# Overflow expert blocks worked in three tiles of 32 rows, and four y buffers in place of two

## The chip, the cores and the metric

The kernel runs on one core of a Trainium2 chip. TensorE (PE) multiplies, VectorE (DVE), ScalarE (ACT) and GpSimd (POOL) work beside it, SyncE (SP) only issues transfers, and 16 DMA engines carry them. The metric is the device time of one launch in microseconds; lower is better.

## The reference

One layer of a hybrid encoder for 1024 prompt rows and 32 sample rows: a token mixer, attention over 256 memory rows, and a mixture of experts with 32 experts. Everything is float32. The change touches the last part only, which is:

```
h  = silu(xr @ w_gate[e]) * (xr @ w_up[e])       # xr: rows of one block, 1024 wide; h: 512 wide
yb = h @ w_down[e]                               # 1024 wide
y  = zeros.at[tok].add(yb * gate)                # each row goes to its top-2 experts
x  = layer_norm(alpha * x + y)
```

Each of the 1056 rows goes to two experts, with a routing that depends on the data.

## The kernel before

**Blocks.** Every expert e = 0..31 gets one block of C = 96 rows, that is NS = 3 tiles of 32 rows. Rows beyond 96 of an expert go to overflow ("spilled") blocks of the same size, of which there can be up to 22. With these inputs there are two, called block 32 (j = 0) and block 33 (j = 1) here. A block needs w_gate, w_up and w_down of its expert, 2 MB each.

**What runs on each engine.** The order is written out by hand, engine by engine, with semaphores between them; each engine works its list strictly in order.

- PE, `step`: gate_up(e), 192 matmuls of the trace (L785), then down(e-1), 96 of them (L794). The output of gate_up takes two PSUM banks, 0 and 1 or 2 and 3 by parity (`B_U`), that of down banks 4 and 5 or 6 and 7 (`B_Y`). Down waits for `h_ready` from DVE.
- ACT, `act_step`: one Exp over the three tiles of gate_up(e) (L1284), then `y_rows(e-1)`: wait until down is done and until the y buffer is free (`y_out`), three scalings of 128x256 (`scale_y`, L1263), four stores to DRAM (`store_y`, L1268). There are two y buffers, so block e waits for the stores of block e-2.
- DVE, `dve_expert`: transposes x of block e+1 (L1756), then four operations of silu over 128x384 (L1743, L1745, L1747, L1749) and one transposition (L1753), which releases down(e).
- SP: loads of gate and up of e+2 when gate_up(e) is done, of down of e+2 when down(e) is done (L1002, L1003, L1007).
- POOL gathers the x rows of a block from DRAM.

**The overflow blocks** come after block 31, each engine in a function `spilled(j, b)` under an `If`. PE: gate_up(b), then the wait for `o_h`, then down(b). ACT waits first, ahead of block 32, for all y stores of the 32 experts; then per block: Exp over three tiles (L1306), wait for down, scale, store, wait until the stores have landed, one small copy (L1313). DVE as in the main loop. SP: gate and up of block 32 when gate_up(30) is done, of block 33 when gate_up(31) is done; down of each when down(30) or down(31) is (L1028, L1029, L1034).

**After them** ACT signals `fin_ready` (L1326). POOL then gathers every row's two y rows from DRAM (L1967), and the last layer norm follows tile by tile.

```
act.wait_ge(y_done, e + 1)
act.wait_ge(gate_ready, e + 1)
wait_count(act, y_out[b], 64 * j)
scale_y(b).then_inc(y_ready, 1)
act.wait_ge(y_ready, e + 1)
store_y(y_dram[bass.ds(e * C, C), :], b, y_out[b], 16)
```

Of the kernel before, what the change touches and what calls it, by code (L numbers as in the profile page):

```python
# [23 lines left out]
NE = G * EG  # L24
DE = 512
KE = DE // P
C = 96
NS = C // 32
# [4 lines left out]
BANK = 512  # L33
# [16 lines left out]
def build(nc, io):  # L50
    ctx = ExitStack()
    with ctx:
        def sem(name):
            return ctx.enter_context(nc.semaphore(name))
# [46 lines left out]
        gate2 = const(2 * NS).rearrange("p (b a) -> p b a", a=NS)  # L101
# [7 lines left out]
        R = MIX + KD * T  # L109
# [70 lines left out]
        gu = [view(a, "m k n", m=2, k=KD, n=DE) for a in EXP]  # L180
        wd = [view(a + 8192, "k n", k=KE, n=D) for a in EXP]
# [92 lines left out]
        y_out = [sem(f"y_out{i}") for i in range(2)]  # L274
# [5 lines left out]
        o_gate = sem("o_gate")  # L280
# [125 lines left out]
        def _(pe):  # L406
            mm = nc.tensor.matmul
# [418 lines left out]
            pe.wait_ge(tables_ready, 1)  # L826
            n_over = pe.value_load(over_i[0:1, NOVER:NOVER + 1], min_val=0, max_val=NOVER)

            def spilled(j, b, turn_n):
                pe.wait_ge(o_xt, j + 1)  # L830
                pe.wait_ge(o_w[b], 32 * turn_n + 32)
                gate_up(b).then_inc(o_gu, 1)
                pe.wait_ge(o_h, j + 1)
                pe.wait_ge(o_down[b], 16 * turn_n + 16)
                if isinstance(j, int):
                    pe.wait_ge(y_ready, NE - 1 + j)
                else:
                    pe.wait_ge(o_y, 65 * j - 129)
                down(b).then_inc(o_dn, 1)

            with pe.If(n_over > 0):
                spilled(0, 0, 0)
# [10 lines left out]
        def _(sp):  # L853
# [168 lines left out]
            def spilled(j, b):  # L1022
                e = sp.value_load(over_i[0:1, bass.ds(j, 1)], min_val=0, max_val=NE - 1)
                if isinstance(j, int):
                    sp.wait_ge(gu_done, NE - 1 + j)
                else:
                    sp.wait_ge(o_gu, j - 1)
                sp.dma_start(gu[b][:, 0], dyn(gate_w, e)).then_inc(o_w[b], 16)  # L1028
                sp.dma_start(gu[b][:, 1], dyn(up_w, e)).then_inc(o_w[b], 16)  # L1029
                if isinstance(j, int):  # L1030
                    sp.wait_ge(y_done, NE - 1 + j)
                else:
                    sp.wait_ge(o_dn, j - 1)
# [19 lines left out]
            sp.wait_ge(mem_out, 16)  # L1053
            for i in range(2):
                sp.wait_ge(state_out[i], 32 * HH // 2)
                sp.wait_ge(y_out[i], 64 * NE // 2)


        @block.scalar
        def _(act):  # L1060
# [200 lines left out]
            def scale_y(b):  # L1261
                for a in range(NS):
                    last = A(ye[:, b, a, :], B_Y[b][:, a * 256:(a + 1) * 256], ACT.Copy, scale=gate2[:, b, a:a + 1])  # L1263
                return last

            def store_y(rows, b, s, n):
                for q in range(4):
                    act.dma_start(rows[:, 256 * q:256 * q + 256].rearrange("(a t) n -> t a n", t=32),  # L1268
                                  ye[32 * q:32 * q + 32, b]).then_inc(s, n)

            def y_rows(e, b, j):

                act.wait_ge(y_done, e + 1)
                act.wait_ge(gate_ready, e + 1)
                wait_count(act, y_out[b], 64 * j)
                scale_y(b).then_inc(y_ready, 1)
                act.wait_ge(y_ready, e + 1)
                store_y(y_dram[bass.ds(e * C, C), :], b, y_out[b], 16)

            def act_step(e, b, j, first=False):  # L1280
                act.wait_ge(gu_done, e + 1)
                if not first:
                    act.wait_ge(h_ready, e)
                A(sg, gate_rows[b], ACT.Exp, scale=-1.0).then_inc(g_exp, 1)  # L1284
                if not first:
                    y_rows(e - 1, 1 - b, j + b - 1)

            act_step(0, 0, 0, first=True)
            act_step(1, 1, 0)
            act_step(2, 0, 1)  # L1290
            with act.Fori(1, NE // 2 - 1) as i:
                act_step(2 * i + 1, 1, i)
                act_step(2 * i + 2, 0, i + 1)
            act_step(NE - 1, 1, NE // 2 - 1)
            y_rows(NE - 1, 1, NE // 2 - 1)

            act.wait_ge(tables_ready, 1)
            n_over = act.value_load(over_i[0:1, NOVER:NOVER + 1], min_val=0, max_val=NOVER)

            def spilled(j, b):  # L1300
                act.wait_ge(o_gu, j + 1)
                if isinstance(j, int) and j == 0:
                    act.wait_ge(h_ready, NE)
                else:
                    act.wait_ge(o_h, j)
                A(sg, gate_rows[b], ACT.Exp, scale=-1.0).then_inc(g_exp, 1)  # L1306
                act.wait_ge(o_dn, j + 1)
                act.wait_ge(o_gate, j + 1)
                scale_y(b).then_inc(o_y, 1)
                act.wait_ge(o_y, 65 * j + 1)  # L1310
                store_y(y_dram[bass.ds(j * C + NE * C, C), :], b, o_y, 16)
                act.wait_ge(o_y, 65 * j + 65)
# [8 lines left out]
            with act.If(n_over > 2):  # L1321
                with act.Fori(1, NOVER // 2) as i:
                    for b in range(2):
                        with act.If(2 * i + b < n_over):
                            spilled(2 * i + b, b)
            A(rstd[:, 1:2], eps_ln, ACT.Copy).then_inc(fin_ready, 1)  # L1326

            for t in range(NT):
# [13 lines left out]
        def _(dve):  # L1342
# [409 lines left out]
            def turn_h(b):  # L1752
                return V.transpose(hhT[:, b], hh.rearrange("p s (d k) -> p s k d", k=KE))  # L1753
# [34 lines left out]
            def spilled(j, b, turn_n):  # L1788
                dve.wait_ge(o_x[b], 16 * NS * turn_n + 16 * NS)
                turn_x(b).then_inc(o_xt, 1)  # L1790
                dve.wait_ge(g_exp, j + NE + 1)
                silu_up(b, 4 * j + 4 * NE)
                if isinstance(j, int):
                    dve.wait_ge(y_done, NE - 1 + j)
                else:
                    dve.wait_ge(o_dn, j - 1)
                turn_h(b).then_inc(o_h, 1)
                if isinstance(j, int):
                    dve.wait_ge(y_ready, NE - 1 + j)
                else:  # L1800
                    dve.wait_ge(o_y, 65 * j - 129)
# [204 lines left out]
```

## Time and profile before

| | us |
|---|---|
| median of 3 runs | 1997.67 (1995.52 to 1998.9) |
| the profiled execution | 1996.47 |
| its span on the core | 1994.1 |
| PE busy | 1792.5 (90%) |
| DVE busy | 750.0 (38%) |
| ACT busy | 309.1 (16%) |

Times in rows are microseconds from the start of the span. "<-" behind an idle time names what ended it. The transfers' GB/s and the share of the 16 DMA engines say whether the memory side is full: over the expert stage, from about 1360 to 1885, it is.

### The profile page before, as it was taken

The numbers are of one execution on the slowest core, as the hardware profiler recorded it, in microseconds if no ns is written. First come the engines' busy times: TensorE is split into PE (matmuls) and PEld (weight loads), VectorE is DVE, ScalarE is ACT, GpSimd is POOL, SyncE is SP. The second block draws the span as 40 slices with busy tenths as digits, with TensorE's granted clock in tenths as the row PEclk, the third lists the DMA queues.
The fourth block names the chain that finished last, engine by engine and source line by source line (L and its number), as shares of the span: only waits on it lengthen the run. The fifth ranks groups of instructions, "written<-read, shape, count | busy, mean of one in ns | idle before, by whom it ended". The sixth has DMA issues, their size and how long they took to land. (4 is left out here: it accounts for less than half of the span.)

```text
span 1994.1 us, 33667 instructions
## 1 busy us (share of the span) xinstructions
PE 1792.5 (90%) x14867; PEld 1131.6 (57%) x14867; DVE 750.0 (38%) x1089; ACT 309.1 (16%) x701; POOL 210.5 (11%) x196
## 2 busy tenths in 40 slices
PE   8999999999999779999998999939999999999650
PEld 4455568766654554445665665426666666666420
DVE  1111456534461653320012443364433333333227
ACT  1111223411010440111001111000101111111005
POOL 2100000000010420000000000032111111111016
PEclk9999999999999689999999999859999999999875
DMA  5341002001100203045111000349999999999826
GB/s 197 96 165 43 1 5 83 1 1 43 42 0 4 92 6 116 33 136 169 34 42 42 22 22 28 144 171 366 422 424 424 424 425 423 424 424 424 360 61 216
DMA packets 72862, 326.94 MB, mean 164 GB/s; under 512 B 13368, under 2 KB 27968, under 8 KB 59728
## 3 DMA queue, kind: packets, MB, share of 16 engines
q1 hardware_dynamic: 47840, 280.70, 35.1%
q10 hardware_dynamic: 17360, 22.03, 3.4%
q0 software_dynamic: 7584, 23.08, 3.2%
q8 instruction: 61, 1.00, 0.2%
q14 instruction: 17, 0.14, 0.0%
HBM read 288.05 MB, written 37.65 MB: 163 GB/s over the span
## 5 line engine op out<-in xcount | busy, mean ns | idle before, releaser
L785 PE MATMUL psum<-arena 128*32 128x256 f32 x6528 | 360.4, 380 | 32.0 <-issue 30.8
L418 PE MATMUL psum<-arena 128*128 128x352 f32 x1152 | 342.1, 460 | 0.0
L785 PEld LDWEIGHTS psum<-arena 128*32 128x32 f32 x6528 | 244.7, 110 | 146.5 <-issue 45.4
L427 PE MATMUL psum<-arena 128*128 128x512 f32 (+1 forms) x720 | 318.4, 601 | 5.9 <-DMA arena<-in_w_in 4.7
L418 PEld LDWEIGHTS psum<-arena 128*128 128x128 f32 x1152 | 219.3, 191 | 122.2 <-issue 1.1
L1348 DVE COPY arena<-psum 128x512 f32<-128x512 f32 (+7 forms) x135 | 90.9, 681 | 417.8 <-PE psum L427 221.6
L427 PEld LDWEIGHTS psum<-arena 128*128 128x128 f32 (+1 forms) x720 | 131.7, 185 | 177.4 <-issue 175.5
L794 PE MATMUL psum<-arena 128*32 128x256 f32 x3264 | 189.7, 389 | 24.1 <-DVE arena L1753 24.1
L794 PEld LDWEIGHTS psum<-arena 128*32 128x32 f32 x3264 | 125.4, 113 | 82.0 <-DVE arena L1753 25.5
L1743 DVE TENSOR_SCALAR arena<-arena 128x384 f32<-128x384 f32 x34 | 12.2, 360 | 357.1 <-ACT arena L1284 315.3
L1065 ACT ACTIVATE arena<-psum 128x128 f32<-128x128 f32 (+5 forms) x181 | 86.5, 495 | 349.8 <-PE psum L411 276.2
L1938 POOL DMA_INDIRECT arena<-x_rows,consts x102 | 96.7, 948 | 414.1 <-DVE arena L1756 386.0
L411 PE MATMUL psum<-consts,arena 128*128 128x128 f32 (+4 forms) x819 | 121.8, 280 | 12.4 <-ACT arena L1065 6.3
L411 PEld LDWEIGHTS psum<-consts,arena 128*128 128x128 f32 (+4 forms) x819 | 97.2, 154 | 59.0 <-issue 30.8
L643 PE MATMUL psum<-arena 128*128 128x512 f32 (+1 forms) x288 | 125.3, 593 | 0.0
L1545 DVE SCALAR_TENSOR_TENSOR arena<-arena,psum 128x1024 f32<-128x1024 f32 (+1 forms) x18 | 22.0, 1220 | 185.8 <-PE psum L427 103.8
L1263 ACT ACTIVATE arena<-psum,consts 128x256 f32<-128x256 f32 x102 | 40.9, 471 | 324.0 <-DMA y_blocks<-arena 270.6
L643 PEld LDWEIGHTS psum<-arena 128*128 128x128 f32 (+1 forms) x288 | 51.5, 181 | 68.3 <-issue 67.9
L1745 DVE RECIPROCAL arena<-arena 128x384 f32<-128x384 f32 x34 | 86.8, 2553 | 1.2
L546 PE MATMUL psum<-arena 128*128 128x64 f32 (+2 forms) x624 | 76.5, 266 | 0.0
L511 PE MATMUL psum<-arena 66*128 66x512 f32 (+3 forms) x192 | 75.6, 502 | 0.5 <-DVE consts L1348 0.5
L1118 ACT ACTIVATE arena<-psum,consts 128x128 f32<-128x128 f32 (+8 forms) x72 | 51.3, 713 | 150.5 <-DVE consts L1401 148.7
(243 smaller groups left out, 1402.1 us busy)
## 6 DMA issues: line engine op xcount, KB each, us to landing
arena<-in_moe_w_down SPq DMA_DIRECT2D x34, 2048.0 KB, 22.6
arena<-in_moe_w_gate SPq DMA_DIRECT2D x34, 2048.0 KB, 16.9
arena<-in_moe_w_up SPq DMA_DIRECT2D x34, 2048.0 KB, 22.0
arena<-in_w_in SPq DMA_DIRECT2D x7, 2048.0 KB, 9.8
y_blocks<-arena ACTq DMA_DIRECT2D x136, 96.0 KB, 2.0
y_blocks<-arena ACTq DMA_DIRECT2D x1, 8448.0 KB, 44.0
arena<-in_x_prompt SPq DMA_DIRECT2D x9, 512.0 KB, 3.3
arena<-in_w_out SPq DMA_DIRECT2D x2, 2048.0 KB, 11.0
```

What stands on the lines that cost most here:

```text
L411: return nc.tensor.transpose(out, a, ident[0:n, 0:n])
L418: last = mm(ps[0:m, c * BANK:c * BANK + THIRD], lhs(k), rhs[:, k, c * THIRD:(c + 1) * THIRD], start=(k == 0), stop=(k == KD - 1))
L427: last = mm(ps[0:n, c * 512:(c + 1) * 512], lhs(k), rhs(k, c), start=(k == 0), stop=(k == KD - 1))
L511: last = mm(ps[0:nq, c:e], q, ka[0:KX, h, c:e], start=True, stop=True)
L546: last = mm(ps_o[0:nq, h * FD:(h + 1) * FD], probsT[p][0:w_, u % nbuf, b, 0:nq], v, start=(b == 0), stop=(b == len(blocks) - 1))
L643: last = mm(psum[0:n, b:b + BANK], mixT[:, k, cols_of(t)], wrows[:, k, c * 512:(c + 1) * 512], start=(k == 4), stop=(k == 3))
L785: last = mm(out, xeT[:, b, a, k, :], gu[b][:, :, k, j * P:(j + 1) * P], start=(k == 0), stop=(k == KD - 1))
L794: last = mm(B_Y[b][32 * j:32 * j + 32, a * 256:(a + 1) * 256], hhT[:, b, a, k, :], wd[b][:, k, j * 256:(j + 1) * 256], start=(k == 0), sto ...
L1065: take(A(out, src, ACT.Copy), key)
L1348: take(V.tensor_copy(out, src), key)
L1745: V.reciprocal(sg, sg).then_inc(silu_step, 1)
L1938: pool.indirect_dma_start(out=xe[:, b, a, :], out_offset=None, in_=x2_quarters, in_offset=bass.IndirectOffsetOnAxis(ap=tok_idx[:, e, a:a + ...
```

## The change

**Main loop.** Four y buffers `ye[0..3]` in place of two; block e uses buffer e % 4 and waits for the stores of block e-4. ACT's loop is unrolled by four experts instead of two. Nothing else moves in the main loop.

**Overflow blocks.** Each of the three tiles of gate_up has a bank of its own (3b + a) and its own signal `o_gu`. ACT takes Exp tile by tile (128x128), DVE does the silu and the transposition tile by tile and signals `o_h` three times a block; its small copy of the gate values (L1802 before) now stands ahead of the silu. PE's down waits per tile, writes all blocks' results to banks 6 and 7 (`O_Y`, tiles 0 and 1 in bank 6, tile 2 in bank 7), and signals `o_dn` after tile 1 and after tile 2. ACT scales tiles 0 and 1 after the first signal and tile 2 after the second. The wait for all y stores of the experts moves from ahead of the overflow blocks to behind them; a block waits only for the buffer that it uses. The wait for a block's own stores (`o_out`) stays at the block's end.

```diff
-        ye = view(R + 15360, "a s n", a=2, s=NS, n=256)
+        ye = [view(R + a, "s n", s=NS, n=256) for a in (15360, 16128, 21504, 22272)]
...
             def spilled(j, b, turn_n):
                 pe.wait_ge(o_xt, j + 1)
                 pe.wait_ge(o_w[b], 32 * turn_n + 32)
-                gate_up(b).then_inc(o_gu, 1)
-                pe.wait_ge(o_h, j + 1)
-                pe.wait_ge(o_down[b], 16 * turn_n + 16)
...
+                for a in range(NS):
+                    for k in range(KD):
+                        for q in range(4):
+                            out = psum[32 * q:32 * q + 32, (3 * b + a) * BANK:(3 * b + a) * BANK + 256]
...
+                    last.then_inc(o_gu, 1)
+                pe.wait_ge(o_down[b], 16 * turn_n + 16)
...
+                for a in range(NS):
+                    pe.wait_ge(o_h, 3 * j + a + 1)
...
+                    if a > 0:
+                        last.then_inc(o_dn, 1)
...
             def spilled(j, b):
-                act.wait_ge(o_gu, j + 1)
...
+                for a in range(NS):
+                    act.wait_ge(o_gu, 3 * j + a + 1)
+                    A(sg[:, a, :], psum[:, (3 * b + a) * BANK:(3 * b + a) * BANK + P], ACT.Exp, scale=-1.0)\
+                        .then_inc(g_exp, 1)
                 act.wait_ge(o_gate, j + 1)
...
-            for i in range(2):
-                act.wait_ge(y_out[i], 64 * (NE // 2))
             with act.If(n_over > 0):
                 spilled(0, 0)
```

**How the lists differ.** ACT, from the end of the main loop through the first overflow block. Before, with the branch into block 32 behind the stores of both buffers:

```order
L1263 ACTIVATE arena<-psum,consts 128x256 [waits y_out1,gate_ready,y_done]
L1263 ACTIVATE arena<-psum,consts 128x256 x2
L1268 DMA y_blocks<-arena 32x3x256 [waits y_ready]
L1268 DMA y_blocks<-arena 32x3x256 x3
L1298 TENSOR_LOAD consts [waits tables_ready]
L1298 ISA x2
L1317 COMPARE_AND_BRANCH [waits y_out1,y_out0]
L1306 ACTIVATE arena<-psum 128x384 [waits h_ready,o_gu]
```

The same place in the changed kernel:

```order
L1289 ACTIVATE arena<-psum,consts 128x256 [waits y_out3,gate_ready,y_done]
L1289 ACTIVATE arena<-psum,consts 128x256 x2
L1280 DMA y_blocks<-arena 32x3x256 [waits y_ready]
L1280 DMA y_blocks<-arena 32x3x256 x3
L1312 TENSOR_LOAD consts [waits tables_ready]
L1312 ISA x2
L1338 COMPARE_AND_BRANCH
L1323 ACTIVATE arena<-psum 128x128 [waits o_gu,h_ready]
L1323 ACTIVATE arena<-psum 128x128 [waits o_gu] x2
L1330 ACTIVATE arena<-psum,consts 128x256 [waits y_out0,o_dn,o_gate]
```

The wait on y_out has left the branch and stands on the first scaling; the Exp is in three parts.

PE, the first overflow block, before and now:

```order
-L785 MATMUL psum<-arena 32x256 [waits o_w0,o_xt]
-L785 MATMUL psum<-arena 32x256 x95
-L794 MATMUL psum<-arena 32x256 [waits y_ready,o_down0,o_h]
-L794 MATMUL psum<-arena 32x256 x47
```

```order
+L840 MATMUL psum<-arena 32x256 [waits y_ready,o_w0,o_xt]
+L840 MATMUL psum<-arena 32x256 x95
+L852 MATMUL psum<-arena 32x256 [waits o_h,y_ready,o_down0]
+L852 MATMUL psum<-arena 32x256 x15
+L852 MATMUL psum<-arena 32x256 [waits o_h]
+L852 MATMUL psum<-arena 32x256 x15
+L852 MATMUL psum<-arena 32x256 [waits o_h]
+L852 MATMUL psum<-arena 32x256 x15
```

The matmuls and their order are the same (each of the listing is two MATMULs of the trace); the wait for `o_h` stands at three places instead of one.

## Rows read from the trace of the kernel before

**Rows 1.** Busy time by stretch: length, engines, granted clock, DMA share, GB/s.

```profile
1600.00:1700.00 100.00, 94.53 (x1736) 67.16 (x1732) 38.64 (x42) 9.44 (x23) 17.04 (x19) 1.00 1.01 424
...
1864.00:1866.00 2.00, 0.00 (x0) 0.00 (x0) 1.90 (x4) 0.00 (x0) 0.00 (x0) 0.65 1.10 438
...
1886.00:1888.00 2.00, 0.00 (x0) 0.00 (x0) 0.00 (x0) 0.13 (x1) 0.00 (x0) 1.00 0.29 106
...
1890.00:1892.00 2.00, 0.00 (x0) 0.00 (x0) 0.00 (x0) 0.00 (x0) 0.00 (x0) 0.50 0.89 192
```

**Rows 2.** DMA queues, 1500 to 1533.32: packets, MB, share; q1 SP's, q10 ACT's.

```profile
q1 hardware_dynamic: 864, 12.58, 88.8%
q10 hardware_dynamic: 864, 0.76, 6.6%
```

**Rows 3.** Timeline of PE, the end of the expert stage: start, duration, what.

```profile
1845.85 10.57 PE L785 MATMUL psum<-arena 128*32 128x256 f32 x192 [1.18 <-DMA arena<-in_moe_w_up]
1856.21 5.39 PE L794 MATMUL psum<-arena 128*32 128x256 f32 x96
1866.40 7.84 PE L794 MATMUL psum<-arena 128*32 128x256 f32 x96 [4.80 <-DVE arena L1753]
1874.07 10.53 PE L785 MATMUL psum<-arena 128*32 128x256 f32 x192
1898.22 7.30 PE L794 MATMUL psum<-arena 128*32 128x256 f32 x96 [13.62 <-DVE arena L1753]
1905.34 10.54 PE L785 MATMUL psum<-arena 128*32 128x256 f32 x192
1921.55 7.58 PE L794 MATMUL psum<-arena 128*32 128x256 f32 x96 [5.67 <-DVE arena L1753]
```

**Rows 4.** Timeline of ACT, two places of the expert stage and its end.

```profile
1478.54 1.20 ACT L1263 ACTIVATE arena<-psum,consts 128x256 f32<-128x256 f32 x3 [5.05 <-DMA y_blocks<-arena]
...
1860.80 0.49 ACT L1284 ACTIVATE arena<-psum 128x384 f32<-128x384 f32 x1 [2.17 <-issue]
1875.15 1.20 ACT L1263 ACTIVATE arena<-psum,consts 128x256 f32<-128x256 f32 x3 [13.86 <-DMA y_blocks<-arena]
...
1892.63 0.49 ACT L1306 ACTIVATE arena<-psum 128x384 f32<-128x384 f32 x1 [3.56 <-DMA y_blocks<-arena]
...
1934.95 0.20 ACT L1326 ACTIVATE consts<-consts 128x1 f32<-128x1 f32 x1
```

**Rows 5.** Groups of DVE instructions by shape: busy us, mean ns.

```profile
L1745 DVE RECIPROCAL arena<-arena 128x384 f32<-128x384 f32 x34 | 86.8, 2553 | 1.2
L1756 DVE STREAM_TRANSPOSE arena<-arena 128x768 f32<-128x768 f32 x34 | 54.3, 1596 | 8.5 <-DMA arena<-x_rows,consts 8.3
L1753 DVE STREAM_TRANSPOSE arena<-arena 128x384 f32<-128x384 f32 x34 | 30.0, 883 | 1.2
L1439 DVE RECIPROCAL arena<-arena 128x1056 f32<-128x1056 f32 x4 | 27.0, 6753 | 0.1
...
L1400 DVE TENSOR_TENSOR psum<-psum,consts 128x128 f32<-128x128 f32 x64 | 19.1, 298 | 61.5 <-PE psum L511 61.5
...
L1743 DVE TENSOR_SCALAR arena<-arena 128x384 f32<-128x384 f32 x34 | 12.2, 360 | 357.1 <-ACT arena L1284 315.3 <-ACT arena L1306 41.8
```

**Rows 6.** SP's loads of w_up for blocks 32 and 33: issues, and the second's landing.

```profile
1847.40 0.38 SPq L1029 DMA_DIRECT2D arena<-in_moe_w_up  x1
...
1863.29 1.53 SPq L1029 DMA_DIRECT2D arena<-in_moe_w_up  x1
...
DMA to landing us min/median/max: 19.6/19.6/19.6
```

**Rows 7.** SP early on, timeline: a load and a store behind others.

```profile
90.04 0.55 SPq L894 DMA_DIRECT2D arena<-in_w_in  x1
...
93.34 22.33 SPq L900 DMA_DIRECT2D out_fox_k_s<-arena  x1
```

**Rows 8.** DMA issues between 80 and 135: that first load of them, KB, us to landing.

```profile
arena<-in_w_in SPq DMA_DIRECT2D x1, 2048.0 KB, 29.6
```

More of the change, by code:

```diff
@@ L273, in build @@
         xe_in = [sem(f"xe_in{i}") for i in range(2)]
-        y_out = [sem(f"y_out{i}") for i in range(2)]
+        y_out = [sem(f"y_out{i}") for i in range(4)]
         gu_done, y_done = sem("gu_done"), sem("y_done")
@@ L831, in spilled @@
                 pe.wait_ge(o_w[b], 32 * turn_n + 32)
-                gate_up(b).then_inc(o_gu, 1)
-                pe.wait_ge(o_h, j + 1)
-                pe.wait_ge(o_down[b], 16 * turn_n + 16)
                 if isinstance(j, int):
                     pe.wait_ge(y_ready, NE - 1 + j)
-                else:
-                    pe.wait_ge(o_y, 65 * j - 129)
-                down(b).then_inc(o_dn, 1)
+                for a in range(NS):
+                    for k in range(KD):
+                        for q in range(4):
+                            out = psum[32 * q:32 * q + 32, (3 * b + a) * BANK:(3 * b + a) * BANK + 256]
+                            last = mm(out.rearrange("p (m n) -> p m n", m=2), xeT[:, b, a, k, :],
+                                      gu[b][:, :, k, q * P:(q + 1) * P], start=(k == 0), stop=(k == KD - 1))
+                    last.then_inc(o_gu, 1)
+                pe.wait_ge(o_down[b], 16 * turn_n + 16)
+                if isinstance(j, int) and j == 0:
+                    pe.wait_ge(y_ready, NE)
+                else:
+                    pe.wait_ge(o_y, j)
+                for a in range(NS):
+                    pe.wait_ge(o_h, 3 * j + a + 1)
+                    for k in range(KE):
+                        for q in range(4):
+                            last = mm(O_Y[32 * q:32 * q + 32, a * 256:(a + 1) * 256], hhT[:, b, a, k, :],
+                                      wd[b][:, k, q * 256:(q + 1) * 256], start=(k == 0), stop=(k == KE - 1))
+                    if a > 0:
+                        last.then_inc(o_dn, 1)
             with pe.If(n_over > 0):
@@ L1055, in _ @@
                 sp.wait_ge(state_out[i], 32 * HH // 2)
-                sp.wait_ge(y_out[i], 64 * NE // 2)
+            for i in range(4):
+                sp.wait_ge(y_out[i], 64 * NE // 4)
         @block.scalar
@@ L1259, in _, with store_y @@
                          for a in (0, 2)]
[L1261 to L1266, printed above, removed]
+            def store_y(rows, slot, s):
                 for q in range(4):
                     act.dma_start(rows[:, 256 * q:256 * q + 256].rearrange("(a t) n -> t a n", t=32),
-                                  ye[32 * q:32 * q + 32, b]).then_inc(s, n)
@@ L1271, in y_rows @@
-            def y_rows(e, b, j):
+                                  ye[slot][32 * q:32 * q + 32]).then_inc(s, 16)
+            def y_rows(e, b, slot, turn_n):
                 act.wait_ge(y_done, e + 1)
                 act.wait_ge(gate_ready, e + 1)
-                wait_count(act, y_out[b], 64 * j)
-                scale_y(b).then_inc(y_ready, 1)
+                wait_count(act, y_out[slot], 64 * turn_n)
+                for a in range(NS):
+                    last = A(ye[slot][:, a, :], B_Y[b][:, a * 256:(a + 1) * 256], ACT.Copy, scale=gate2[:, b, a:a + 1])
+                last.then_inc(y_ready, 1)
@@ L1277, in y_rows, with act_step @@
                 act.wait_ge(y_ready, e + 1)
-                store_y(y_dram[bass.ds(e * C, C), :], b, y_out[b], 16)
-            def act_step(e, b, j, first=False):
+                store_y(y_dram[bass.ds(e * C, C), :], slot, y_out[slot])
+            def act_step(e, r, turn_n):
                 act.wait_ge(gu_done, e + 1)
-                if not first:
+                if not isinstance(e, int) or e > 0:
                     act.wait_ge(h_ready, e)
-                A(sg, gate_rows[b], ACT.Exp, scale=-1.0).then_inc(g_exp, 1)
-                if not first:
-                    y_rows(e - 1, 1 - b, j + b - 1)
@@ L1288, in _ @@
[L1288 to L1295, printed above, removed]
+                A(sg, gate_rows[r % 2], ACT.Exp, scale=-1.0).then_inc(g_exp, 1)
+                if not isinstance(e, int) or e > 0:
+                    y_rows(e - 1, (r - 1) % 2, (r - 1) % 4, turn_n)
@@ L1297, in _ @@
+            for e in range(7):
+                act_step(e, e % 4 + 4, (e - 1) // 4)
+            with act.Fori(1, NE // 4 - 1) as i:
+                for r in range(3, 7):
+                    act_step(4 * i + r, r, i if r < 5 else i + 1)
+            act_step(NE - 1, NE - 1, NE // 4 - 1)
+            y_rows(NE - 1, 1, 3, NE // 4 - 1)
             act.wait_ge(tables_ready, 1)
             n_over = act.value_load(over_i[0:1, NOVER:NOVER + 1], min_val=0, max_val=NOVER)
+            O_Y = psum[:, 6 * BANK:8 * BANK]
@@ L1304, in spilled @@
                 else:
-                    act.wait_ge(o_h, j)
-                A(sg, gate_rows[b], ACT.Exp, scale=-1.0).then_inc(g_exp, 1)
-                act.wait_ge(o_dn, j + 1)
-                act.wait_ge(o_gate, j + 1)
[L1309 to L1312, printed above, removed]
+                    act.wait_ge(o_h, 3 * j)
+                for a in range(NS):
+                    act.wait_ge(o_gu, 3 * j + a + 1)
+                    A(sg[:, a, :], psum[:, (3 * b + a) * BANK:(3 * b + a) * BANK + P], ACT.Exp, scale=-1.0)\
+                        .then_inc(g_exp, 1)
+                act.wait_ge(o_gate, j + 1)
+                act.wait_ge(o_dn, 2 * j + 1)
+                if isinstance(j, int):
+                    act.wait_ge(y_out[b], 64 * NE // 4)
+                for a in range(2):
+                    A(ye[b][:, a, :], O_Y[:, a * 256:(a + 1) * 256], ACT.Copy, scale=gate2[:, b, a:a + 1])
+                act.wait_ge(o_dn, 2 * j + 2)
+                A(ye[b][:, 2, :], O_Y[:, 512:768], ACT.Copy, scale=gate2[:, b, 2:3]).then_inc(o_y, 1)
+                act.wait_ge(o_y, j + 1)
+                store_y(y_dram[bass.ds(j * C + NE * C, C), :], b, o_out)
+                act.wait_ge(o_out, 64 * j + 64)
                 A(lnv[:, 0:1], eps_ln, ACT.Copy)
-            for i in range(2):
-                act.wait_ge(y_out[i], 64 * (NE // 2))
             with act.If(n_over > 0):
@@ L1325, in _ @@
                             spilled(2 * i + b, b)
+            for i in range(4):
+                act.wait_ge(y_out[i], 64 * NE // 4)
             A(rstd[:, 1:2], eps_ln, ACT.Copy).then_inc(fin_ready, 1)
```

31 lines of the change are left out of this document (20 added, 11 removed).

## Prediction

> **What bounds the kernel now.** I read the busy time by stretch first. Over the expert stage the 16 DMA engines are full (share 1.01) at 424 GB/s, and 1736 matmuls in 100 us are 6.03 experts of 288, so 16.6 us each [rows 1]. PE is busy 94.5% of it and waits for weights only. A block moves 6.29 MB of weights, 0.39 MB of y and about as much of x: 7.08 MB / 424 GB/s is 16.7 us. The main loop is bound by bytes, and the change moves none of them. I count no gain there, though the chain of waits puts y stores first.
>
> Then the timeline of PE. From the end of gate_up(31) at 1856.4 its three idle stretches are 4.80, 13.62 and 5.67 us, all ended by DVE's transposition of h [rows 3]. The timeline of ACT says why. Block 28's stores land only at 1875.15, block 5's landed at 1478.54: 396.6 us for 23 blocks, so a set of stores is served every 17.2 us, while blocks come every 16.6 [rows 1, 4]. With two buffers ACT falls behind; it takes Exp(31) at 1860.80, 4.4 us after gate_up(31). Then it holds Exp(32) until every y store has landed, 1892.63, though gate_up(32) was done at 1884.6. The end of the path is `fin_ready` at 1934.95; from it 59.15 us of gathers and layer norm follow to 1994.1, and 2.37 us lie outside the span.
>
> **How the y stores are served.** In 33.32 us the queue of ACT got exactly as many packets as that of SP, 864 and 864 [rows 2]. Its 0.76 MB are 1.93 sets of 0.393 MB, so a set is 447 packets, 28 for each engine, and takes 17.2 us, which agrees with the landings. So the y queue gets one packet for each weights packet, however many sets stand in it. I take it that blocks 28 and 29 land when they did, and the sets queued behind them only after the weights.
>
> The Trainium skill, page "DMA: Bandwidth & Descriptors", section "Queues, rings and completion order", says that each DMA engine goes round robin over the queues that have work, a packet at a time. The trace agrees, 864 to 864. By this rule a deeper y queue gets no larger share, which speaks against this change; were the shares by need instead, block 32's stores would land some 2 us after their issue, and the sum would be the 1967 of the first rival.
>
> **Part by part, from 1856.4 on.**
>
> 1. Four buffers. Exp(31) no longer waits. DVE then takes Exp 0.5 us and silu 5.0 us (for block 31: Exp at 1860.80, down(31) at 1866.40, 5.6 us in all [rows 3, 4]). H is there at 1862.1, down(31) starts 0.5 us after down(30), at 1862.1. PE pauses 0.5 instead of 4.8 us. In that pause the granted clock fell, 0.65 of full in 1864 to 1866 [rows 1], and down(31) took 7.84 us where 5.39 is the time at 2.4 GHz [rows 1, 3]. In the main loop pauses of 0.9 us leave the clock at 1.00, so I take 5.39 (5.18 from start to start, the last matmul overlapping). Down(31) ends at 1867.5: 6.7 us gained.
>
> 2. Gate_up(32) needs x turned (DVE 1.6 us behind the silu, 1863.9) and w_up of block 32, which was issued at 1847.40 and, if it takes the 19.6 us of the next one, lands at 1867.0 [rows 6]. Both are there. It ends at 1877.9, 6.7 us early.
>
> 3. Tiles. Per tile DVE pays, by the 384- and 1056-column rows of the reciprocal, 2553 - 256 x 6.25 = 953 ns; the two products 298 each by the 128-column row; the scalar addition at most 360, some 230; the transposition between 883/3 and 883, by the slope to 768 columns 408 [rows 5]. With gaps 2.33 us. A tile of gate_up takes 3.45 us of PE, so only the last one's chain is open: 0.2 + 0.3 (Exp) + 2.33 = 2.8 us after gate_up. Down's first two tiles cover 3.45 us of that. Down(32) then follows at once: 13.6 us of idle time and 2.1 us of slow clock go [rows 3]. It would end at 1883.1 instead of 1905.4.
>
> 4. Issue of the stores. More sets now stand in ACT's queue. Before, at most two did, 56 packets for each engine, and no issue was held. When block 31 is issued, at 1871, there are 3.1 (served by then: up to part of 28). Early in the kernel such a queue does fill: SP had two transfers of 64 packets for each engine in its queue and was held 22.33 us in the third, until 115.67, with the first landing at 119.64 [rows 7, 8]. So the queue takes about 64 to 72 packets for each engine beyond which the issue is held. Block 31's last of four stores needs 88 - 7 = 81 to fall to 64 or 72: 9 to 17 packets at 1.6 per us are 5 to 10 us. ACT comes to Exp(32) at 1876 to 1881 instead of 1871; silu of three tiles follows, 7.3 us, and down(32) ends at 1885.4 to 1890.6. The row is of another queue; zero is the lower end. I take 1887.
>
> 5. Gate_up(33) needs w_up of block 33, landing at 1863.29 + 19.6 = 1882.9 [rows 6], and x turned, which comes with the last tile of h. It runs 1887 to 1897.5 in my middle case.
>
> 6. The new wait that counts: ACT does Exp(33) only when block 32's own stores have landed (`o_out`), as before, but now blocks 29 to 32 stand in the queue when the weights end at about 1886. Three and a half sets at 106 to 192 GB/s, the rates just behind the weights and of block 31's alone [rows 1], beside each other some 6 to 10 us: landing at 1892.5 to 1896. I take 1893.5. Exp at that time, the three tiles of silu one after another, 7.3 us, and the last tile of down 1.8 us: 1902.6; by gate_up(33) itself 1897.5 + 2.8 + 1.8 = 1902.1. The two delays of 4 and 6 cover each other. With half a microsecond for clock, down(33) ends at 1903.2, against 1929.1 [rows 3].
>
> 7. Scaling: one of three scalings stays behind the last matmul: 0.8 us gained (1.20 to 0.47 by the row of three [rows 4]). The stores and their landing are as before.
>
> Sum: 25.9 + 0.8 = 26.7 us. 1996.47 - 26.7 = 1969.8; the median of the runs shown is 1.2 higher, so **1971**. Costed at nothing: SP's loads (only down(33) is issued earlier, and it queues behind w_up), ACT's longer loop body, the moved copy on DVE (its two waits are met at 1863 and 1869), and the final waits on y_out, met by then. If PE's down found its weights late it would show: w_down of 33 is needed at 1897 and lands by 1888.
>
> **The rivals.**
>
> - No delay of the y stores (steps 4 and 6 cost nothing): gate_up(33) from 1883.1 to 1893.6, down(33) ends at 1898.2 to 1899.2. That is 4 us less, **1967**. For it: ACT's queue never showed a held issue, and step 6's rate is only bounded. Against: the equal packet counts. Chance 0.17.
> - The queue holds only two sets, as much as the trace shows in it: block 31's stores go in at about 1886, when the weights end. Then Exp(32) at 1886, down(32) ends 1895.3, gate_up(33) 1905.7, down(33) 1910.3: 7.1 us more, **1978**. In the main loop ACT would then be held in the issue instead of the wait. Chance 0.15.
> - The tiles don't overlap: the waits stand in PE's list but h comes late, so that 5.6 us stay behind each gate_up. Against it is DVE's 2.33 us a tile against PE's 3.45. With the clock then slow in both downs, 2 x 5.6 + 4.4 less the cover of step 6 leaves about 10 us more: **1981**, with the rival before 1987. Chance 0.06.
> - Slower than before: ACT no longer lags, so x, y and weights all want the DMA engines at the same time throughout, and each block's period grows. The price of the gain is 26.7 us over some 26 blocks of a full loop, so it decides from 1.03 us a block, 6%, or 0.44 MB of extra traffic at 424 GB/s, more than a whole set of y a block. With twice that, **2024**. Against: the y queue is never empty before either, and bytes don't change. At most the two sets that come earlier cost 2 us once. Chance 0.03.
>
> **How the numbers follow.** The forecast 1971 has 0.57 (its own span 1968 to 1975), the rivals 0.17, 0.15, 0.06 and 0.03, and 0.02 are for nothing gained. 1964.5 to 1979 takes in the forecast, the first two rivals with 2 us for the loop, and leaves out 0.11 and some of the tails. A run of this kernel can tell 0.2%, 4 us: faster 0.95, same 0.02, slower 0.03.
>
> **What the profile would show.** ACT's Exp of every block 0.2 us after its gate_up, down(31) within 1 us of down(30) and 5.4 us long, the main loop still 16.6 us a block. Down(32) directly behind gate_up(32) is step 3 without step 4; a store issue of several us in ACT at 1870 is step 4. ACT's first Exp of block 33 after a wait for a DMA at 1892 to 1896 is step 6. I am wrong if the period in the loop moves by more than 0.1 us, if block 32's stores land before 1889 or after 1898, or if the granted clock is not 1.00 up to gate_up(33).

## The result and the profile after

| | before | after |
|---|---|---|
| median, us | 1998.29 (4 runs) | 1970.38 (4 runs: 1967.48 to 1971.37) |
| ratio | | 0.9856, 95% interval 0.9844 to 0.9868 |
| profiled execution, us | 1996.47 | 1967.48 |
| its span, us | 1994.1 | 1965.7 |
| end of gate_up(31), from the span's start | 1856.4 | 1856.8 |
| `fin_ready` | 1934.95 | 1907.07 |
| from there to the end | 59.15 | 58.63 |

The kernel is 1.4% faster, 27.9 us by the medians. In the two profiled executions `fin_ready` comes 27.9 us earlier, and up to the end of gate_up(31) nothing has moved by more than 0.4 us. So the gain lies between two points of the program that were 78.5 us apart and are 50.3 now.

The busy time by stretch in the middle of the main loop, with the columns of [rows 1]:

```profile
1600.00:1700.00 100.00, 94.55 (x1736) 67.24 (x1732) 38.63 (x42) 10.15 (x24) 17.09 (x19) 1.00 1.01 424
```

This is the first line of [rows 1] over again: 1736 matmuls in 100 us, DMA full at 424 GB/s. The queues of SP and ACT, 1500 to 1533.32, still get equal counts of packets, to be laid beside [rows 2]:

```profile
q1 hardware_dynamic: 865, 12.60, 88.9%
q10 hardware_dynamic: 865, 0.76, 6.6%
```

The end of the expert stage is where the two traces differ. PE's timeline, from gate_up(31) on, to be laid beside [rows 3]; L840 is gate_up and L852 down of an overflow block:

```profile
1846.19 10.57 PE L785 MATMUL psum<-arena 128*32 128x256 f32 x192 [1.19 <-DMA arena<-in_moe_w_up]
1856.55 5.39 PE L794 MATMUL psum<-arena 128*32 128x256 f32 x96
1862.42 5.39 PE L794 MATMUL psum<-arena 128*32 128x256 f32 x96 [0.48 <-DVE arena L1776]
1867.63 10.54 PE L840 MATMUL psum<-arena 128*32 128x256 f32 x192
1879.19 1.93 PE L852 MATMUL psum<-arena 128*32 128x256 f32 x32 [1.02 <-DVE arena L1833]
1881.28 1.93 PE L852 MATMUL psum<-arena 128*32 128x256 f32 x32 [0.15 <-DVE arena L1833]
1883.46 1.93 PE L852 MATMUL psum<-arena 128*32 128x256 f32 x32 [0.24 <-DVE arena L1833]
1885.21 10.54 PE L840 MATMUL psum<-arena 128*32 128x256 f32 x192
1895.57 5.36 PE L852 MATMUL psum<-arena 128*32 128x256 f32 x96
```

The idle stretches of 4.80, 13.62 and 5.67 us are 0.48, 1.41 (in three parts) and none. The three downs that took 7.3 to 7.8 us take 5.4, or three times 1.93, because the clock no longer falls; in the stretch that holds the pause before down(31) it is granted in full, where [rows 1] had 0.65:

```profile
1862.00:1864.00 2.00, 1.57 (x32) 0.98 (x36) 1.48 (x3) 1.20 (x3) 0.00 (x0) 1.00 1.00 422
```

ACT's timeline of the same stretch, to be laid beside [rows 4]: L1299 is Exp(31), L1280 the store issues, L1323 Exp of a tile, L1336 the small copy behind a block's own stores.

```profile
1856.82 0.49 ACT L1299 ACTIVATE arena<-psum 128x384 f32<-128x384 f32 x1 [10.55 <-PE psum L785]
...
1863.23 2.98 ACTq L1280 DMA_DIRECT2D y_blocks<-arena  x4
...
1869.11 6.37 ACTq L1280 DMA_DIRECT2D y_blocks<-arena  x4
1876.44 0.45 ACT L1323 ACTIVATE arena<-psum 128x128 f32<-128x128 f32 x2 [7.35 <-issue]
1878.24 0.28 ACT L1323 ACTIVATE arena<-psum 128x128 f32<-128x128 f32 x1 [1.36 <-PE psum L840]
...
1891.46 0.20 ACT L1336 ACTIVATE consts<-consts 128x1 f32<-128x1 f32 x1 [5.53 <-DMA y_blocks<-arena]
...
1895.82 0.28 ACT L1323 ACTIVATE arena<-psum 128x128 f32<-128x128 f32 x1 [3.18 <-PE psum L840]
...
1906.44 0.20 ACT L1336 ACTIVATE consts<-consts 128x1 f32<-128x1 f32 x1 [4.97 <-DMA y_blocks<-arena]
1907.07 0.20 ACT L1349 ACTIVATE consts<-consts 128x1 f32<-128x1 f32 x1 [0.42 <-issue]
```

Exp(31) follows its gate_up at once. The four issues of block 31's stores take 6.37 us, one of them 4.53. Exp(32) comes at 1876.44, 5 us after its first tile was there. The wait for block 32's own stores ends at 1891.5, but the last tile's Exp waits for PE alone.

### The profile page after: what moved, and what is told of

The parts are those of the page before. It is cut to its first block and busy times, and to the rows that moved or that the text cites. A ratio compares the mean times of both kernels' runs of the same rounds, so it can differ in the third digit from the quotient of the medians.

```text
span 1965.7 us, 33639 instructions
## 1 busy us (share of the span) xinstructions
PE 1787.5 (91%) x14867; PEld 1130.0 (57%) x14867; DVE 756.5 (38%) x1109; ACT 309.8 (16%) x705; POOL 209.9 (11%) x196
## 5 line engine op out<-in xcount | busy, mean ns | idle before, releaser
L785 PE MATMUL psum<-arena 128*32 128x256 f32 x6144 | 339.3, 380 | 31.9 <-issue 30.7
L785 PEld LDWEIGHTS psum<-arena 128*32 128x32 f32 x6144 | 232.0, 110 | 138.1 <-issue 45.1
L794 PE MATMUL psum<-arena 128*32 128x256 f32 x3072 | 172.4, 379 | 0.5 <-DVE arena L1776 0.5
L794 PEld LDWEIGHTS psum<-arena 128*32 128x32 f32 x3072 | 117.2, 110 | 49.3 <-DVE arena L1776 1.0
L1768 DVE RECIPROCAL arena<-arena 128x384 f32<-128x384 f32 x32 | 81.7, 2553 | 1.1
L546 PEld LDWEIGHTS psum<-arena 128*128 128x128 f32 (+2 forms) x624 | 72.5, 186 | 2.3 <-issue 1.0
```

Source lines behind the costliest of these rows:

```text
L546: last = mm(ps_o[0:nq, h * FD:(h + 1) * FD], probsT[p][0:w_, u % nbuf, b, 0:nq], v, start=(b == 0), stop=(b == len(blocks) - 1))
L1768: V.reciprocal(sg, sg).then_inc(silu_step, 1)
```

## The experiments

Eleven kernels beside the one on trial. Times are medians; the kernel before was measured beside each group, at 1998.1 to 1998.8.

| kernel | us | ratio to before, 95% interval |
|---|---|---|
| buffers only | 1994.4 | 0.9973 (0.9947 to 0.9998) |
| buffers, moved wait, no tiles | 1985.2 | 0.9930 (0.9913 to 0.9946) |
| tiles and moved wait, two buffers | 1985.3 | 0.9932 (0.9915 to 0.9949) |
| the whole change, early wait put back | 1983.8 | 0.9923 (0.9906 to 0.9939) |
| the whole change, three buffers | 1975.2 | 0.9877 (0.9860 to 0.9895) |
| the whole change | 1970.4 | 0.9856 (0.9841 to 0.9871) |
| own stores waited for later | 1969.8 | 0.9856 (0.9841 to 0.9871) |
| block 31's stores from SP | 1969.9 | 0.9855 (0.9840 to 0.9870) |
| both | 1967.4 | 0.9843 (0.9829 to 0.9856) |
| both, block 33's stores from two queues | 1965.0 | 0.9832 (0.9819 to 0.9846) |
| block 29's stores left out | 1968.5 | one execution |
| the stores of blocks 4 to 27 left out | 1946.8 | 0.9746 (0.9731 to 0.9760) |

### The four buffers alone

The main loop of the changed kernel, the overflow blocks of the one before.

```diff
-            for i in range(2):
-                act.wait_ge(y_out[i], 64 * (NE // 2))
+            for i in range(4):
+                act.wait_ge(y_out[i], 64 * (NE // 4))
             with act.If(n_over > 0):
                 spilled(0, 0)
```

> The kernel before with the four y buffers and ACT's new main loop, and nothing else: the overflow blocks whole, behind the wait for all y stores. Theory (the gain is at the end of the expert stage, and the loop is bound by bytes): down(31) starts 0.5 us after down(30) and gate_up(32) ends at about 1878, but Exp(32) still waits for block 31's stores, landing at about 1890, where it was 1892.6: some 3 us faster than before, 1995, and the period of the main loop unchanged at 16.6 us. Rival (the y stores at the head of the chain of waits are what bounds the loop): most of the 28 us come with the buffers, 1972 to 1980.

Measured: 1994.4. The first line is of its chain of waits, the others of PE and ACT:

```profile
PE 36%; DVE 4%; issue 2%; DMA 2%; POOL 1%; ACT 0%; ACTq 0%; DVEq 0%; SPq 0%; POOLq 0%
```

```profile
1867.79 10.57 PE L785 MATMUL psum<-arena 128*32 128x256 f32 x192
1896.40 6.90 PE L794 MATMUL psum<-arena 128*32 128x256 f32 x96 [18.04 <-DVE arena L1753]
```

```profile
1890.81 0.49 ACT L1304 ACTIVATE arena<-psum 128x384 f32<-128x384 f32 x1 [21.81 <-DMA y_blocks<-arena]
```

In the kernel before, the chain's first item was DMA with 21%, all of it y_blocks. Here that item is gone from the chain; and the time fell by 4 us, since gate_up(32) came 6 us earlier and then waited 18 us. The stores were at the head of the chain because ACT always had one to wait for, not because anything waited for ACT. The rival falls.

### Two buffers, with the tiles

```diff
-        ye = [view(R + a, "s n", s=NS, n=256) for a in (15360, 16128, 21504, 22272)]
+        ye = [view(R + a, "s n", s=NS, n=256) for a in (15360, 16128)]
```

> The changed kernel with two y buffers and the main loop of before: the tiles and the moved wait alone. Theory: ACT still lags, Exp(31) at 1860.8, block 31's scaling waits for block 29's stores until 1887.9, so Exp(32) comes at about 1891, h of its last tile 7.3 us later, down(32) ends at 1900, gate_up(33) at 1910.4, down(33) at 1915: 14 to 15 us faster than before, 1984. Rival (the buffers add nothing to the tiles): 1970, as the whole change.

Measured: 1985.3, as expected. ACT comes to Exp(32) when block 31's stores have at last been issued:

```profile
1887.05 1.20 ACT L1280 ACTIVATE arena<-psum,consts 128x256 f32<-128x256 f32 x3 [12.62 <-DMA y_blocks<-arena]
1888.28 1.77 ACTq L1285 DMA_DIRECT2D y_blocks<-arena  x4
1891.00 0.61 ACT L1326 ACTIVATE arena<-psum 128x128 f32<-128x128 f32 x3 [2.75 <-issue]
```

### The buffers and the moved wait, without tiles

```diff
-            for i in range(4):
-                act.wait_ge(y_out[i], 64 * (NE // 4))
             with act.If(n_over > 0):
...
                 act.wait_ge(o_gate, j + 1)
+                if isinstance(j, int):
+                    act.wait_ge(y_out[b], 64 * NE // 4)
```

> Four buffers and the moved wait, the overflow blocks whole as before. Theory: Exp(32) follows gate_up(32) at 1878.2, silu takes 5.0 us in one piece, down(32) starts at 1883.7, gate_up(33) ends at 1899.6, down(33) starts at 1905.2 and ends at 1910.6 to 1912.8 by its clock: 16 to 18 us faster than before, 1981, so that the tiles are worth about 10 us of the whole. Rival (the tiles add only instructions, the waits were the cost): 1971.

Measured: 1985.2, 4 us more than expected. PE's two downs of the overflow blocks:

```profile
1885.22 7.91 PE L794 MATMUL psum<-arena 128*32 128x256 f32 x96 [5.65 <-DVE arena L1755]
...
1909.15 7.89 PE L794 MATMUL psum<-arena 128*32 128x256 f32 x96 [5.66 <-DVE arena L1755]
```

The pauses are those that were expected, the durations are not: both downs are slow, 2.5 us each, where the expectation counted a slow clock in the second at most. gate_up(31) also starts 1 us later in this execution than in the changed kernel's, for reasons ahead of the change. The tiles are thus worth 14.8 us on top of the rest: 11.3 us of pauses less the 1.4 that stay, and 5.0 of clock.

### The early wait put back

```diff
+            for i in range(4):
+                act.wait_ge(y_out[i], 64 * NE // 4)
             with act.If(n_over > 0):
                 spilled(0, 0)
```

> The changed kernel with the wait for all y stores put back ahead of the overflow blocks. Theory: Exp(32) at about 1890, when block 31's stores have landed; tile by tile on DVE 7.3 us, down(32) ends at 1899.5, gate_up(33) at 1910, down(33) at 1914.5: 13 to 14 us slower than the whole change, 1984. Rival (the wait costs nothing with four buffers, since the stores would have landed): 1971.

Measured: 1983.8, 13.4 us more than the whole change. ACT's first three tiles come all at once, 21 us after its last work:

```profile
1892.96 0.61 ACT L1323 ACTIVATE arena<-psum 128x128 f32<-128x128 f32 x3 [21.07 <-DMA y_blocks<-arena]
```

The four kernels show how the parts stand to each other. Alone, the buffers bring 4 us; the tiles and the moved wait, with two buffers, bring 13; all three together 28. Take any one of the three away and 13 to 15 us are lost, so they add up to more than their single shares. The reason is that ACT reaches Exp(32) early only if it neither waits for a buffer nor for all stores.

The tiles need that least. With four buffers and the early wait they still bring 10.6 us (1994.4 to 1983.8), since the pause of 5.67 us and the slow clock ahead of down(33) go in any case; with the moved wait they bring 14.8. The moved wait brings 9.2 us without the tiles and 13.4 with them. The 4 us between these pairs are less than the 5 us to which the time with the buffers alone is known. The tiles alone, and the moved wait alone, with two buffers each, weren't run.

### Three buffers

Block 31 and both overflow blocks use the buffers of blocks 28, 29 and 30; ACT's loop is written out in full.

```diff
-                    y_rows(e - 1, (r - 1) % 2, (r - 1) % 4, turn_n)
+                    y_rows(e - 1, (e - 1) % 2, (e - 1) % 3, (e - 1) // 3)
```

> The changed kernel with three y buffers, ACT's loop written out in full. Theory: backlog is 2.5 sets in the loop, so three buffers never make ACT wait there by much; only block 31 waits, for block 28's stores landing at 1875.2, which is when its issue ended in the changed kernel anyway: within 1.5 us of the whole change, 1970 to 1972. Rival (the fourth buffer is what lets ACT run free): ACT lags in the loop and the time is 1975 or more.

Measured: 1975.2, 4.8 us slower than the whole change. The theory missed. The time is the rival's, but its mechanism isn't there: ACT didn't lag in the loop.

```profile
1879.13 1.21 ACT L1289 ACTIVATE arena<-psum,consts 128x256 f32<-128x256 f32 x3 [12.52 <-DMA y_blocks<-arena]
1880.37 2.60 ACTq L1280 DMA_DIRECT2D y_blocks<-arena  x4
1883.90 0.61 ACT L1325 ACTIVATE arena<-psum 128x128 f32<-128x128 f32 x3 [3.56 <-issue]
```

```profile
1871.04 10.54 PE L840 MATMUL psum<-arena 128*32 128x256 f32 x192
1886.65 8.23 PE L852 MATMUL psum<-arena 128*32 128x256 f32 x96 [5.07 <-DVE arena L1835]
```

In the loop ACT never waited for a buffer. For block 31 the buffer did come free when block 28's stores landed, but scaling and issue, 1.2 and 2.6 us, stand behind that, while a full queue lets the issue end as soon as there is room. Exp(32) comes 12.9 us after the start of gate_up(32), in the changed kernel 8.8. And the pause of 5.07 us costs the clock in down(32), 8.23 us instead of 5.4. The expectation left both out. So the fourth buffer serves the last block of the loop; in the loop before it nothing waited for a buffer.

### Block 29's stores left out

The y rows of block 29 are zeros here, written at the start.

```diff
-                store_y(y_dram[bass.ds(e * C, C), :], slot, y_out[slot])
+                if e != 29:
+                    store_y(y_dram[bass.ds(e * C, C), :], slot, y_out[slot])
```

> The changed kernel without the stores of block 29's y rows (they are zeros, set early), ACT's loop written out in full. With them the four issues of block 31's stores took 6.37 us. Theory (the issue is held because the queue is full, 88 packets for each engine): with 60 packets there they take 1.8 to 3 us, and Exp(32) comes at 1871 to 1873 instead of 1876.4. Rival (the issue is slow because SP issues loads at that time, or since the instructions are new there): still 6 us.

Measured in one execution, 1968.5 us:

```profile
1865.44 2.87 ACTq L1281 DMA_DIRECT2D y_blocks<-arena  x4
1870.13 1.20 ACT L1290 ACTIVATE arena<-psum,consts 128x256 f32<-128x256 f32 x3 [4.72 <-PE psum L794]
1871.37 1.79 ACTq L1281 DMA_DIRECT2D y_blocks<-arena  x4
1874.09 0.28 ACT L1326 ACTIVATE arena<-psum 128x128 f32<-128x128 f32 x1 [2.75 <-PE psum L840]
```

Block 31's issues take 1.79 us, and Exp(32) follows its tile at once. SP issues the same loads at the same time here, and the instructions are as new. What held the issue was how much stood in ACT's own queue. Whether the limit counts packets or stores stays open: in the six traces with four buffers in which ACT issued block 31's stores behind all of those before, the held issue ended 29.3 to 30.5 us behind the start of gate_up(31), and block 28's stores landed 29.3 us behind it in the kernel before and 29.5 with three buffers. Not every long issue is of this kind. Block 30's 2.87 us stand here and there, about a microsecond more than in the loop; they took 2.60 in the kernel before, which had only two buffers. Block 32's took 3.25 us, and 3.3 to 4.3 where block 29's or block 31's weren't in the queue. What these have in common the runs don't show.

### Where the two remaining delays lie

Two edits and both together. In the first, block 32's own stores are waited for only ahead of block 33's; in the second, SP issues block 31's stores behind its last loads.

```diff
-                act.wait_ge(o_out, 64 * j + 64)
...
+                if isinstance(j, int) and j == 1:
+                    act.wait_ge(o_out, 64)
                 store_y(y_dram[bass.ds(j * C + NE * C, C), :], b, o_out)
```

```diff
+            sp.wait_ge(y_ready, NE)
+            for q in range(4):
+                sp.dma_start(y_dram[(NE - 1) * C:NE * C, 256 * q:256 * q + 256].rearrange("(a t) n -> t a n", t=32),
+                             ye[3][32 * q:32 * q + 32]).then_inc(y_out[3], 16)
```

> The changed kernel itself, beside the three variants of this group: 1970 us, 28 us faster than before.

> The changed kernel with block 32's wait for its own stores moved behind block 33's scaling. Theory: the first Exp of block 33 comes at 1889 instead of 1891.6, but the last tile's Exp waits for gate_up(33) in both, so nothing is gained: within 0.5 us of the changed kernel. Rival (this wait holds the path): 2 to 3 us faster.

> The changed kernel with block 31's stores issued by SP behind its last loads, so that ACT is free at 1869. Theory (the full queue holds ACT, which holds Exp(32)): Exp(32) at 1871.3, down(32) follows gate_up(32) at once and ends at 1883.1, gate_up(33) starts at 1883.4 with w_up's landing: 1.8 us faster than the changed kernel. Rival (the held issue is hidden): no difference, or slower since these stores now stand before the output stores of SP.

> Both of the last two. Theory: with gate_up(33) 1.8 us earlier the wait for block 32's own stores comes nearer to the path, so both together give 1.8 to 2.3 us. Rival: the landing of block 32's stores was never near, and it is as the one with SP alone.

Measured: 1970.4, 1969.8, 1969.9 and 1967.4. The executions differ by 1 to 2 us ahead of the expert stage's end, so the traces are best compared from the start of gate_up(31) to the end of down(33): 54.7 and 55.5 us in two executions of the changed kernel, 55.3 with the late wait, 54.3 with SP's stores, 52.9 with both. With SP's stores alone down(32) follows gate_up(32) at once and gate_up(33) starts 37.0 us after gate_up(31), where it was 39.0 and 39.8. Then the other wait takes most of it back:

```profile
1883.30 10.54 PE L840 MATMUL psum<-arena 128*32 128x256 f32 x192
1894.46 1.93 PE L852 MATMUL psum<-arena 128*32 128x256 f32 x32 [0.62 <-DVE arena L1838]
1896.56 1.93 PE L852 MATMUL psum<-arena 128*32 128x256 f32 x32 [0.16 <-DVE arena L1838]
1898.74 1.93 PE L852 MATMUL psum<-arena 128*32 128x256 f32 x32 [0.24 <-DVE arena L1838]
```

With both edits no down waits:

```profile
1870.03 10.54 PE L840 MATMUL psum<-arena 128*32 128x256 f32 x192
1880.39 5.36 PE L852 MATMUL psum<-arena 128*32 128x256 f32 x96
1885.77 10.57 PE L840 MATMUL psum<-arena 128*32 128x256 f32 x192
1896.12 5.39 PE L852 MATMUL psum<-arena 128*32 128x256 f32 x96
```

So each delay hides the other, as step 6 of the prediction said: removing one gives 0.6 us or less, both 2 to 3. The expectation for the stores from SP, 1.8 us faster, missed: Exp(32) and gate_up(33) did come as it said, but it didn't follow the path on to down(33), which then waited 1.02 us. By the intervals the step from 1970.4 to 1967.4 is at the edge of what the timing tells, and the steps of half a microsecond are below it; the lines of the traces are the better witness.

### Block 33's stores from two queues

On top of both:

```diff
+                sp.wait_ge(o_y, 2)
+                stores(NE + 1, 1, (2, 3), o_out)
...
-                store_y(y_dram[bass.ds(j * C + NE * C, C), :], b, o_out)
+                if isinstance(j, int) and j == 1:
+                    for q in range(2):
+                        act.dma_start(y_dram[(NE + 1) * C:(NE + 2) * C, 256 * q:256 * q + 256].rearrange("(a t) n -> t a n", t=32),
+                                      ye[1][32 * q:32 * q + 32]).then_inc(o_out, 16)
```

> The variant with both edits (block 31's stores from SP, block 32's own stores waited for later), and block 33's four stores issued two by ACT and two by SP. Theory: the four issues behind the last scaling take 1.77 us in ACT, two take 0.9: another 0.9 us off, 1966.5. Rival (the landing of about 3 us behind them sets the end, whoever issues): no difference to 1967.4.

Measured: 1965.0, five of the six executions between 1963.6 and 1966.7.

```profile
1918.21 0.47 ACT L1345 ACTIVATE arena<-psum,consts 128x256 f32<-128x256 f32 x1 [0.84 <-PE psum L852]
1918.71 0.86 ACTq L1349 DMA_DIRECT2D y_blocks<-arena  x2
1921.62 0.20 ACT L1355 ACTIVATE consts<-consts 128x1 f32<-128x1 f32 x1 [2.94 <-DMA y_blocks<-arena]
```

From the last scaling's end to the copy behind the stores it is 2.94 us instead of the changed kernel's 4.97. The issues give 0.9 of that, as expected (1.77 to 0.86). The other 1.1, a shorter landing behind the last issue, can't be put down to the second queue. In the kernel with block 32's late wait, where ACT issued all four in 1.79 us, the landing was shorter still, 3.45 less 1.79:

```profile
1906.28 0.20 ACT L1339 ACTIVATE consts<-consts 128x1 f32<-128x1 f32 x1 [3.45 <-DMA y_blocks<-arena]
```

Over the thirteen traces in which ACT issued all four stores of block 33 this stretch ran from 3.45 to 5.16 us. The intervals of this kernel and of the one with both edits overlap, so the 2.4 us between the medians show a gain at most, not its size. By the median it is the fastest version with all stores, 1.7% under the kernel before.

Its profiled execution is the sixth, 1982.8 us long. Gate_up(31) starts at 1865.30 there instead of 1845 to 1850 in the others that store every block. The loss lies ahead of the expert stage, in code that no variant changes. From about 249 to 287 us the granted clock was 0.50, its lower level of 1.2 GHz, while PE was busy without a pause and nothing moved by DMA:

```profile
260.00:280.00 20.00, 20.00 (x63) 14.09 (x63) 8.72 (x20) 4.35 (x12) 0.00 (x0) 0.50 0.00 1
```

In the same stretch the changed kernel ran 108 matmuls at 1.00. Some 38 us at half the clock lose about 19 us (an estimate from these numbers), which is the delay. Why the clock fell there is open.

### The stores of blocks 4 to 27 left out

Zeros stand in their place, written at the start.

```diff
-                store_y(y_dram[bass.ds(e * C, C), :], slot, y_out[slot])
+                if not 4 <= e < 28:
+                    store_y(y_dram[bass.ds(e * C, C), :], slot, y_out[slot])
```

> The changed kernel without the stores of the y rows of blocks 4 to 27 (zeros stand there, set early), ACT's loop written out in full. Theory (the loop is bound by bytes): 6.69 MB a block at 424 GB/s are 15.8 us instead of 16.66, PE's own work is 15.6, so a period of 15.6 to 15.8 and some 20 us less over 24 blocks: 1950. The y queue is empty by block 31, so no issue is held. Rival (PE or the order of the loads sets the period): 16.66 us a block still, and 1968.

Measured: 1946.8, ratio 0.9746 (0.9731 to 0.9760), 3 us less than expected.

```profile
1600.00:1700.00 100.00, 99.61 (x1828) 70.63 (x1821) 43.88 (x49) 10.69 (x27) 17.00 (x18) 1.00 1.01 423
```

DMA is as full as before, at 423 GB/s, and 1828 matmuls pass in 100 us instead of 1736: 15.75 us a block, where 6.69 MB / 424 GB/s is 15.8. PE is busy 99.6%, so it stands at the edge of its own work. The y stores do cost the loop 0.9 us a block, by their bytes; when they are issued, or how long they take to land, costs it nothing. That is why the buffers moved nothing there. 24 blocks of 0.9 us are 22 of the 23.6 us gained. Of the rest, 1.6 to 2.4 us lie behind the start of gate_up(31), from which it is 53.1 us to the end of down(33) instead of 54.7 and 55.5: block 31's issues take 1.76 us, and down(32) follows gate_up(32) at once.

## Why the prediction was right

It forecast 1971; 1970.38 was measured, and none of its three signs of being wrong came: as many matmuls pass in 100 us of the loop, block 32's stores land at 1891.5, and the granted clock is 1.00 up to gate_up(33). The path and the mechanism are as forecast; that the number is off by only 0.6 us is in part luck, since steps 4 and 6 were too slow by 2.3 us together and step 7 too fast by 1.0. Step by step, in the changed kernel's profiled execution:

- **The loop** was costed at nothing, and its period is unchanged. Shown from both sides: by the buffers alone, 4 us, and by the stores left out.
- **Step 1**, down(31) at 1862.1 and 5.39 us long: 1862.42 and 5.39.
- **Step 2**, gate_up(32) to end at 1877.9: 1878.2.
- **Step 3**, the tiles. The costs of DVE at 128 columns were drawn from wider rows. Measured, count and mean in ns:

```profile
L1827 DVE RECIPROCAL arena<-arena 128x128 f32<-128x128 f32 x6 | 5.7, 953 | 0.2
...
L1833 DVE STREAM_TRANSPOSE arena<-arena 128x128 f32<-128x128 f32 x6 | 2.5, 412 | 0.2
...
L1829 DVE TENSOR_TENSOR arena<-arena,psum 128x128 f32<-128x128 f32 x6 | 1.7, 287 | 0.2
...
L1825 DVE TENSOR_SCALAR arena<-arena 128x128 f32<-128x128 f32 x6 | 1.2, 199 | 19.1 <-ACT arena L1323 19.1
```

  The slopes of [rows 5] gave 953, 408, 298 and 230. A tile takes 2.20 us, 2.33 was said.
- **Step 4**, the held issue, was a step that no row of this stage showed; it came from a stall of another queue at 93 us [rows 7, 8]. It is there, 6.37 us instead of 1.77, and is proved by block 29's stores left out. The size was a little high: Exp(32) at 1876.4 lies at the near end of 1876 to 1881, and down(32) ends at 1885.4, where 1887 was taken. The queue took more than the 64 to 72 packets for each engine that were estimated. By the step's own working the fourth store found 81, and 4.53 us at 1.6 packets a microsecond are 7 of them, so it was taken at some 74. Counted from the other end, if block 28's stores land just then, as they did at 1875.15 before, three sets of 28 less the 7 of the held store are 77. So the estimate from these numbers is 74 to 77 ahead of the held store. The step said that no issue was held before; that isn't quite so, since one of block 30's took 1.28 us there.
- **The service of the y queue**, one packet for each weights packet however many sets stand in it, decides whether block 29's stores land as before. They were issued from 1846.4 to 1847.9, 12 us before their issue in the kernel before, and the last landed 40.5 us behind (the third number), so at 1888.4, against 1887.9. This supports the step but doesn't prove it: the first of the four is put at 19.0 us, 1865.4, ahead of the 1875.15 at which block 28's landed before, and no run settles that:

```profile
DMA to landing us min/median/max: 19.0/25.1/40.5
```

- **Step 6**, block 32's own stores: landing at 1891.5, where 1893.5 was taken. Its sum doesn't come out: three and a half sets, 1.38 MB, at 106 to 192 GB/s are 7 to 13 us and not 6 to 10. The measured rate was higher, 267, 225 and 56 GB/s in the three stretches of 2 us from 1886 on. The wait held up only the first tile's Exp of block 33. The step said that the two delays cover each other; they do, and this one had no share left in the end. Down(33) ends at 1900.9, where 1903.2 was forecast.
- **Step 7** is the term that was too good. From the end of down(33) to `fin_ready` the prediction counts 5.1 us; it was 6.1. Scaling is 0.8 shorter as said, but the stores land 0.6 us later behind the scaling (4.97 against 4.36 us, which is within the 3.45 to 5.16 us of all traces), and 0.4 us more pass between the two small copies, with four waits and a branch between. 2.3 us too much in steps 4 and 6 and 1.0 too little here make most of the difference: 27.9 us gained in the trace, where the sum said 26.7.

The rivals: the tiles do overlap; the queue holds more than two sets; the y stores are delayed but cost little, so that the first rival's 1967 was reached, with all stores kept, only when both delays were removed by hand. The slower case needed 1 us more a block and got none.

## What to carry to other kernels

The item at the head of a chain of waits can be one that nobody waits for: here 21% of the span vanished from the chain for 4 us of time. Ask of the resource that is full how many bytes the change moves, and look for the gain where that resource runs dry. When an engine must reach a point early, remove every wait ahead of that point at once: with the tiles in place, either wait left standing cost 13 to 15 us of the 28. A queue of transfers is itself a buffer of limited length: a deeper ring of buffers behind a full memory side moves the wait into the issue, unless another engine's queue takes the last stores.

## What the runs showed of the hardware that was not expected

- With some 88 packets for each DMA engine to be queued, ACT's queue held the last store's issue for 4.5 us, until some 74 to 77 stood ahead of it (an estimate, above); with 60 the four issues took 1.79 us.
- Pauses of PE of 4.64 to 5.67 us were each followed by a down of 7.4 to 8.2 us instead of 5.4. After longer ones, of 8.6 to 18 us, it took less, 6.8 to 7.4 us. After pauses of 1.6 us and less a down took 5.4 us, or three times 1.93.
- The same four stores of 96 KB from one queue, with nothing else to move, took 3.45 to 5.16 us from the scaling's end to the copy behind them, from one trace to another.
- In one execution the granted clock fell to 0.50 for some 38 us in the middle of unbroken matmuls, and the time was 18 us longer. Of the 95 executions one more, of the kernel before, was as far out: 2017.11 us, at a mean granted clock of 0.940 instead of 0.948; it left no trace.
